# Block one in head pairs: two softmax tiles per step, two-head stick-breaking units with gate products between them, modulations spread over the program, and x loaded ahead of the small inputs

## The reference, cut to what matters

```
# block one, twice
h = rmsnorm(x, g_pre) @ w_in
a_q, a_k, a_v, b_b, b_c, b_x, c_q, c_kv, c_kr, d_q, d_k, d_v, gate = split(h)
ya = swa_sink_attention(...)        # 4 heads of 64, 2 kv heads, window 128
yb = short_gated_conv(...)
yc = mla(...)                       # 4 heads of 64 + 32 rope, causal softmax
yd = stick_breaking_attention(...)  # 4 heads of 64:
     z = q k^T * scale;  log_keep = log_sigmoid(-z) below the diagonal
     a = exp(log_sigmoid(z) + sum of log_keep over the later keys);  out = a v
y = rmsnorm(stack(ya, yb, yc, yd), g_grp) * silu(gate)
x = x + rmsnorm(y @ w_out, g_post)

# block two, twice
mod_x = silu(c) @ w_mod[i] + b_mod[i]        # 6 vectors of 1024
mod_c = silu(c_ctx) @ w_mod[i] + b_mod[i]    # layer 1: only the first two are used
... attention, Fourier and Hyena mixing, conv FFN, for x (and for ctx in layer 0)
```

## Time and profile before

| what | value |
|---|---|
| median of three runs | 2697.95 us (2692.81 to 2703.16) |
| profiled execution | 2688.22 us, of which the span is 2686.3 us |
| PE busy | 2416.0 us, 90% of the span |
| DVE / ACT / POOL busy | 1650.7 / 1030.2 / 778.6 us |
| DMA | 259.53 MB, mean 97 GB/s |
| chain that ended last | PE 73%, DVE 11%, issue 8%, ACT 5% |

### The profile page before, as it was taken

How to read it: one execution, slowest core, us unless ns; L and a number is a source line. 1 busy time by engine, 2 the same in 40 slices (tenths; PEclk the granted TensorE clock), 3 DMA queues, 4 the chain that set the end, 5 groups by cost and what they waited for, 6 DMA issues and landing times.

```text
span 2686.3 us, 37059 instructions
## 1 busy us (share of the span) xinstructions
PE 2416.0 (90%) x11870; PEld 1860.6 (69%) x11870; DVE 1650.7 (61%) x3180; ACT 1030.2 (38%) x1728; POOL 778.6 (29%) x542
## 2 busy tenths in 40 slices
PE   5999876999977888997998989999979889899996
PEld 3767554866645768996666668888847566688885
DVE  6868768868759666744448455553164672655612
ACT  3333443233443435654325244443243352444421
POOL 2201134211124326663110243333321003333343
PEclk9989988999999899998999999999989999999998
DMA  4523113432222314554120023323322101233231
GB/s 153 189 95 110 63 55 131 157 126 95 79 86 100 125 62 148 180 180 164 48 99 29 11 69 95 101 94 97 105 102 83 67 1 55 63 95 101 94 97 60
DMA packets 71541, 259.53 MB, mean 97 GB/s; under 512 B 7873, under 2 KB 9314, under 8 KB 69444
## 3 DMA queue, kind: packets, MB, share of 16 engines
q1 hardware_dynamic: 71364, 257.42, 28.4%
HBM read 255.29 MB, written 2.10 MB: 96 GB/s over the span
## 4 chain that ended last, share of the span: by engine, by line
PE 73%; DVE 11%; issue 8%; ACT 5%; POOL 1%; DMA 1%; DVEq 0%; ACTq 0%; SPq 0%; POOLq 0%
PE banks L973 7%; PE banks L971 7%; PE banks L967 7%; PE banks L996 4%; PE banks L990 4%; PE banks L989 4%; PE banks L704 3%; PE banks L705 3%; PE banks L709 3%; PE banks L480 2%; PE banks L864 2%; PE banks L481 2%; PE banks L485 2%; PE banks L894 2%; DVE banks L1443 2%
## 5 line engine op out<-in xcount | busy, mean ns | idle before, releaser
L1242 ACT ACTIVATE wh_t<-ring 128x1024 fp32r<-128x1024 f32 x264 | 278.8, 1057 | 488.8 <-PE banks L973 298.0
L1666 DVE TENSOR_TENSOR wl_t<-ring,wh_t 128x512 fp32r<-128x512 f32 x264 | 195.4, 741 | 421.6 <-ACT wh_t L1242 417.0
L1992 POOL TENSOR_TENSOR wl_t<-ring,wh_t 128x512 fp32r<-128x512 f32 x132 | 221.9, 1683 | 509.3 <-ACT wh_t L1242 509.3
L2034 POOL TENSOR_TENSOR wl_t<-ring,wh_t 128x512 fp32r<-128x512 f32 x132 | 237.2, 1797 | 397.7 <-ACT wh_t L1242 397.6
L1443 DVE CUSTOM_DVE_ANT_0 banks<-m_t 128x512 f32<-128x512 f32 x384 | 314.5, 819 | 11.4 <-issue 0.7
L1935 POOL TENSOR_TENSOR wl_t<-ring,wh_t 128x512 fp32r<-128x512 f32 x72 | 110.7, 1540 | 444.5 <-ACT wh_t L1060 444.4
L480 PE MATMUL banks<-xh_t,wh_t 128*128 128x512 f32 x512 | 208.8, 408 | 7.1 <-DVE y_t L1614 5.3
L973 PE MATMUL banks<-xl_t,wh_t 128*128 128x512 f32 (+1 forms) x960 | 203.0, 354 | 0.0
L967 PE MATMUL banks<-xh_t,wh_t 128*128 128x512 f32 (+1 forms) x960 | 203.0, 354 | 0.0
L971 PE MATMUL banks<-xh_t,wl_t 128*128 128x512 f32 (+1 forms) x960 | 203.0, 354 | 0.0
L481 PE MATMUL banks<-xl_t,wh_t 128*128 128x512 f32 x512 | 202.7, 396 | 0.0
(11 more groups left out here) (342 smaller groups left out, 4685.7 us busy)
## 6 DMA issues: line engine op xcount, KB each, us to landing
ring<-w_d SPq DMA_DIRECT2D x338, 512.0 KB, 3.6
m_t<-wmod_d SPq DMA_DIRECT2D x96, 512.0 KB, 3.6
qh_t<-tables_d SPq DMA_DIRECT2D x6, 1024.0 KB, 4.9
m_t<-tables_d SPq DMA_DIRECT2D x6, 1024.0 KB, 7.0
par<-p_d SPq DMA_DIRECT2D x4, 696.0 KB, 5.4
x_t<-x_in_d SPq DMA_DIRECT2D x1, 2048.0 KB, 12.7
big<-tables_d SPq DMA_DIRECT2D x2, 1024.0 KB
out_d<-x_t SPq DMA_DIRECT2D x1, 2048.0 KB, 7.1
```

The costliest lines, as they stand in the source:

```text
L1242: nc.scalar.activation(WH[j % 2], slot2(j), ACT.Copy).then_inc(sm2["w2_hi"], 1)
L2034: pool.tensor_tensor(WL[q % 2][:, 0:512], slot2(24 + q)[:, 0:512], WH[q % 2][:, 0:512].bitcast(F32), ALU.subtract).then_inc(sm2["w2_lo_a"], 1)
```

## The change

Softmax tiles go in pairs. A step has two heads, whose scores go to two banks (3 and 4), transposes to 5 and 6, and both outputs to the two halves of bank 7, copied at once. The sliding-window heads are paired (0,3) and (2,1), so that the two lie on different row halves; the weights are permuted to suit. There are 16 steps instead of 32, and they hold only products 16 to 19, each cut in halves of 12 matmuls (`half_product`), one on each odd step up to 15.

```diff
+                def scores(p):
...
+                    else:
+                        pe.wait_ge(*at("p_exp", 2 * p))
...
+                    for e, t in enumerate(pair):
+                        pe.matmul(ps[3 + e][:, 0:w], t["q"], t["k"], start=True, stop=False)
...
+                pieces = [(j, part) for j in range(16, 20) for part in range(2)]
+                for s in range(TN // 2 + 2):
+                    if s < TN // 2:
+                        scores(s)
...
+                    if s % 2 and pieces:
+                        half_product(*pieces.pop(0))
+                    if 0 <= s - 1 < TN // 2:
+                        probs_t(2 * s - 2)
+                        probs_t(2 * s - 1)
+                    if 0 <= s - 2 < TN // 2:
+                        values_p(s - 2)
```

```diff
+                for u in range(len(U) + 1):
                     if u < len(U):
...
+                        z_scores(u)
+                        half_product(20 + u, 0)
+                    if u in (2, 4, 6):
+                        group_sum(u // 2 - 1)
+                    if u == 5:
+                        stick_values(0)
                     if u >= 1:
...
+                        keep_sums(u - 1)
+                    if u < len(U):
+                        half_product(20 + u, 1)
+                stick_values(1)
```

```diff
+                        nc.vector.tensor_tensor_reduce(out=half_scratch if half else mod_scratch, in0=MRING[r % RM], in1=cbc[:, w * D:(w + 1) * D],
...
+                    if t % 2 == 1 and not is_ctx:
+                        later_modulation(t // 2)
```

```diff
+            for i in range(4):
+                sp.dma_start(x_t[:, 1024 * i:1024 * (i + 1)].rearrange("p (c t) -> p c t", c=2),
+                             x_in[2 * i:2 * i + 2].rearrange("c p t -> p c t")).then_inc(x_loaded[i // 2], 16)
+            for l in range(DEPTH):
...
-            act.wait_ge(x_loaded, 16)
-            with act.Fori(0, DEPTH) as l:
+            act.wait_ge(small_set, 1)
+            for l in range(DEPTH):
...
-            with dve.Fori(0, DEPTH) as l:
+            link_cond = link
+            for l in range(DEPTH):
```

More of the change, by code:

```diff
@@ L112, in counts2 @@
     )
-LINK_DVE2 = {True: 61, False: 93}
+LINK_DVE2 = {True: 61, False: 95}
 START2 = dict(g_ready=2, z2_added=1)
@@ L573, in scores @@
+                def scores(p):
+                    pair = [tile(2 * p + e) for e in range(2)]
+                    if p == 0:
                         pe.wait_ge(*at("vt_copied", 8))
-                    if t["kind"] == "m":
+                    else:
+                        pe.wait_ge(*at("p_exp", 2 * p))
+                    if pair[0]["kind"] == "m":
                         pe.wait_ge(*at("rot_ready", 5))
                         pe.wait_ge(*at("kr_copied", 4))
-                    if i >= 2:
-                        pe.wait_ge(*at("p_exp", i - 1))
@@ L596, in values_p @@
[L596 to L606 removed]
+                    w = pair[0]["n"] * P
@@ new lines, in low_one @@
+                def low_one(i, chunks):
+                    for k in chunks:
+                        pe.wait_ge(*at(("yl_a", "yl_b")[k % 2], k // 2 + 1))
+                        mm = pe.matmul(accs[i], WH[(NH + i) % 2][:, k * P:(k + 1) * P], XL[k], start=False, stop=k == KD - 1)
+                    return mm
+                high_pair(range(3))
+                group_sum(3)
+                high_pair(range(3, 6))
+                low_one(0, range(6))
+                low_one(1, range(6))
+                high_pair(range(6, KD))
@@ L675, in _ @@
+                for i in range(2):
+                    low_one(i, range(6, KD)).then_inc(sm["acc_ready"], 1)
                 for c in range(2, KD):
@@ L1610, in _ @@
-                x_low("yh_ready", "yl_b", Y)
+                        nc.vector.scalar_tensor_tensor(both(sp_ts[hp], k), z_both(w), 0.0, lz_both(u, w),
+                                                       ALU.max, ALU.add).then_inc(sm["sp_done"], 1)
+                        modulation(16 + u)
+                    if u == 0:
+                        for step in range(5, 10):
+                            short_conv(step)
+                    if u in (3, 5, 7):
+                        group_norm(u // 2 - 1)
@@ new lines, in _ @@
+                    if u == 6:
+                        stick_copy(0)
+                        for g in range(4):
+                            gate_product(g)
+                            gated(g)
+                    if u == 7:
+                        gate_product(4)
+                        gated(4)
+                for g in range(5, KD):
+                    gate_product(g)
+                gated(5)
+                y_low(1)
+                stick_copy(1)
+                y_low(3)
+                y_low(5)
```

637 lines of the change are left out of this document (349 added, 288 removed).

## The result

The changed kernel takes 2578.66 us (median of four runs, 2576.27 to 2580.71), the one before 2699.02 in the same comparison: ratio 0.9565, 95% interval 0.9543 to 0.9586, so 120 us less. Forecast were 2552 and a range of 2512 to 2602. The profiled execution took 2576.3 us, which is 111.9 less than that of before; the sum had 145.5 on that scale. So 33.5 us of the expected gain are missing there (27 on the medians, since the profiled run of before lay 9.7 us under its median and that of after 2.4), and they are to be found.

A forecast was written before the change was run, and what follows sets the result against it. PE was taken as nearly always busy, with waits in block one to win; stages -110, layer turns -9 and -4.5, stage 1 -1.5, start -17, end -3.5 sum to -145.5, giving 2552 us, range 2512 to 2602.

The forecast's parts named there:

- signs of being wrong: Either stage passes 100 us, up products stretch, or pair steps' granted clock falls to 0.5 for more than a few us.
- rival (a): Both stages: pair chain longer than read from single tiles, stages 103 and 101 us, time 2599; chance 0.13.
- the forecast's own bounds: Whole kernel: stages 170 to 205 us a layer, others -6 to +20, not all at once: 2515 to 2590.
- The pair chain: Softmax stage: steps bound by scores, DVE and ACT's exponentials, 4.9 us for four key blocks to 2.7, 56 us together.
- 2 for stretches at the lower clock: Softmax stage: 2 us added on the path for PE running at the lower clock.
- the last pair's way: End of softmax stage: last pair's scaling, transposes, copies and values, 3.5 us on the path.
- PE's work: Stick-breaking stage: scores, masks, sums, values, group sums and eight products take PE 86.6 us a layer.
- unit 5: Stick-breaking stage: five sigmoids and two table loads on ACT show here; with the last exponential some 3 us.
- rival (d): Both stages: PE's clock falls to the 1.2 GHz level, making the kernel slower than before, 2800 us; chance 0.02.
- Rival (e): Kernel start: it does not move because parameters or x land late, time 2569; chance 0.04.
- Between the layers: Layer turn: earlier scaling -4.2 us, DVE's loop-turn stall -4.7, taken as -9; block one to two -4.5.
- Modulations: Moved into block two's FFNs: one 1.35 us instruction fits DVE's 2.40 us idle gap, cost 0; uncovered, up to 130.

The follow-up runs named there:

- thin modulations: Changed kernel with all but 8 of 1024 weights left out in each of block two's 96 modulations: 2578.0 us.
- the second execution: The changed kernel profiled again with nothing altered: 2580.9 us, softmax stages 102.9 and 103.3 us.
- copy first: Changed kernel with DVE's copy of pair 14's outputs ahead of a low part and the last short-conv step at softmax step 16: 2576.8 us, again 2561.2.
- low parts last: Changed kernel with DVE's low parts of softmax steps 4, 8 and 12 behind the scaling of the same step's probabilities: 2577.9 us, again 2568.0.
- busy PE: Changed kernel with unread matmuls added behind the MLA products, after value transposes and in softmax steps 0 and 1: 2570.9 us.
- kernel before, unrolled: Kernel before the change with DVE's loop over block one's two layers written out twice: 2691.4 us beside 2685.1, one execution of each.
- serial heads: Changed kernel with each stick-breaking head's mask matmul directly behind that head's scores, so the two heads' scores are separated: 2618.5 us.

## Why the prediction was right, and where its sum was off

**Direction and mechanism.** Right in the main. PE's waits for POOL went, the softmax stage is held by the chain over ACT's exponentials, heads overlap, and moved modulations are hidden (thin modulations).

**By its own signs.** The stages were to show it at 88 to 95 and 87 to 93 us; they took 100.1 and 96.6. Two of the signs of being wrong came: a stage above 100, and a clock of 0.51 for 17.5 us around the first pair steps. The others hold: ACT's exponentials release PE, heads overlap, the first product stands at 21.8 us, DVE does not idle before the second layer's first low part, and the up products take 5.4 us each. The time lies 26.7 us above the forecast and 20.3 below rival (a), so nearer to (a), but inside the forecast's own bounds of 2515 to 2590, as are the two stages (196.7 a layer for 170 to 205).

**The pair chain.** Steps without a half product took 4.8, 4.0, 3.2 and 2.4 us for 4, 3, 2 and 1 key blocks, and 3.5 for a window pair (sum: 4.9, 4.15, 3.4, 2.7). From step 2 to step 14 the stage took 69.0 us where the working adds up to 68, and 71.8 and 72.2 in the second execution, with more of it at the low clock. Rival (a) as a longer chain in every pair is therefore out, but one of its reasons, DVE in program order, holds at single places: the end (4.5 us, copy first) and steps 5, 9 and 13 (3.2 us, low parts last). Its 103 is nearer than 91.

**The two ends of the softmax stage.** Here the step failed that put "2 for stretches at the lower clock", for which it had no row, and 3.5 for "the last pair's way". Steps 0 and 1 took 14.3 us for 9.7 in the working; 3.7 of that is the clock (busy PE). The end took 16.8 for 10.7; 4.5 of that is DVE's order, by the copy first, and with the first stick-breaking scores ahead of the last values it is 9.9 (1.2 of this is the shift told above). The low part and the conv step ahead of the copy could be read from the code; the sum followed the last pair and not the one before it.

**Stick-breaking.** The step that failed is PE's work: 86.6 in the sum, 93.6 in the run (96.6 less the 3.0 that shows besides). A half product costs 2.94 us, not 2.75 (16 of them: 3.0), score pairs 11.8 a layer instead of 8.8, masks about 0.5 instead of 0.42 a pair (1.3). Nearly all of it is the 0.21 us of a change between kinds of matmul, for which the sum had no term and which cutting every product in two pays more often. The earlier trace rows already held it: 1.05 us from one head's scores of 512 columns to the sums, where the columns need 0.84. What was to show besides, 3 us, came in size but half by luck: 1.2 before the last values, as said, and 1.8 from the low clock at the stage's start, which the sum did not have; unit 5, which it did, shows no wait. The mean clock was 0.98, as forecast above 0.95; rival (d) did not come.

**Start.** -17.0 for -17; first product at 21.8 us. Rival (e) is out.

**Between the layers.** -7.8 for -9. The loop turn went (kernel before, unrolled), but what is late next takes part of it back: the scaling waits 1.52 us for the parameters. The sum had said that nothing would.

**Modulations.** 1.35 us was near for a row of 1024 beside an idle POOL: 1.22. The mean is 1.63, as POOL holds it up (below). In the output stage that was paid from gaps, -0.4 and -1.1 us.

**End.** -4.4 for -3.5, with the four transfers.

**Open.** Block two took between 1789 and 1804 us in these executions, and the softmax stage of unchanged code 100.0 to 103.3. The places at low clock move from one execution to the next, of one and the same kernel too, and what moves them was not found.

## What to carry over

Where a tuned kernel trades waits for work on the same engine, count changes between kinds of matmul as well as columns. Follow the last step of a pipelined loop through every engine's program order, since short copies stand behind long waits there. And before work is taken out of a waiting stage, ask whether it is this work that holds the clock: here 84 matmuls taken out of each stage gained next to nothing, and unread ones added in a gap took 3.7 us off the steps behind it.

## What the runs showed of the hardware

- PE's granted clock is part of the schedule. 84 matmuls fewer a layer left a stage of 100 us at 100 us, at clock 0.67 for 0.91; matmuls added for nothing took 3.7 us off two steps (14.3 to 10.6, in both layers of all four executions that have them).
- 0.21 us for each change between float32 matmuls on half and on the full array: 32 more a layer cost 6.8 us (serial heads).
- The turn of a hardware loop over a long body cost 4.73 us on DVE, with nothing to wait for, and the gap went when the loop was unrolled. A gap of 5.58 us stands at the same place on PE (not tested by unrolling).
- A DVE operation that reads two inputs from SBUF stands still while POOL, begun before it, does the same. In the thin modulations an operation on 8 columns takes 0.16 us alone and 1.25 us beside POOL, and ends when POOL's ends:

```profile
1734.66 1.80 POOL L2162 TENSOR_TENSOR wl_t<-ring,wh_t 128x512 fp32r<-128x512 f32 x1 [5.72 <-ACT wh_t L1390]
1735.22 1.26 DVE L2054 CUSTOM_DVE_ANT_0 m_t<-m_t 128x8 f32<-128x8 f32 x1
```

The Trainium skill (SBUF — State Buffer, Who interferes with whom) says that a DVE instruction with two SBUF inputs contends with a GpSimd instruction that reads SBUF, and that issue order decides which of them blocks. These rows agree, and so do 2.3 us for a row of 1024 beside POOL, and DVE's own subtraction that began 0.05 us ahead of POOL's here and took its usual 0.69. The conv step of 1.75 us in the 4.91 us wait is another: the one before it in the sequence, a column longer, takes 0.74 where POOL is idle.
